# A two-block model on one core: output quarters of the second block's mixers in another order, and how the first expert pieces are released

## The reference, cut to what matters

```
h = h + hybrid_mixer(rms_norm(h, g1), w_in, ..., w_out, lb)     # ends in: concat(r_out, h_out) @ w_out  (1024 x 1024)
h = h + expert_choice_ffn(rms_norm(h, g2), w_router, w_gate, w_up, w_down)

def expert_choice_ffn(xn, w_router, w_gate, w_up, w_down):      # 16 experts, each takes 32 tokens
    affinity = softmax(xn @ w_router)
    gate, idx = top_k(swapaxes(affinity, 1, 2), 32)
    xe = xn[idx]
    ye = (silu(xe @ w_gate) * (xe @ w_up)) @ w_down * gate
    return zeros.at[idx].add(ye)
```

## Time and profile before

| | us |
|---|---|
| median of three runs | 1857.3 (1857.11 to 1859.0) |
| profiled execution, its own time | 1856.24 |
| its span, first to last instruction | 1854.4 |

### The profile page before, as it was taken

How to read it: one execution, slowest core, us unless ns; L and a number is a source line. 1 busy time by engine, 2 the same in 40 slices (tenths; PEclk the granted TensorE clock), 3 DMA queues, 4 the chain that set the end, 5 groups by cost and what they waited for, 6 DMA issues and landing times.

```text
span 1854.4 us, 24842 instructions
## 1 busy us (share of the span) xinstructions
PE 1454.0 (78%) x10541; PEld 1069.3 (58%) x10541; DVE 799.2 (43%) x1246; ACT 571.2 (31%) x898; POOL 62.2 (3%) x56
## 2 busy tenths in 40 slices
PE   8999999999999999985555445579999555555546
PEld 7999999989999898861212112149886121111212
DVE  5767777776777799830101001019973010000101
ACT  4655555465554585321000000028532100000001
POOL 1010000010000000100000000002010000000000
PEclk9999999999999999998777778789999877777868
DMA  9426555534655385799999999997479999999997
GB/s 325 145 70 226 191 174 173 171 104 154 199 182 182 110 271 161 294 372 430 429 430 430 430 429 429 430 394 245 153 293 369 430 429 429 430 430 429 430 429 315
DMA packets 165492, 563.14 MB, mean 304 GB/s; under 512 B 12600, under 2 KB 116534, under 8 KB 137606
## 3 DMA queue, kind: packets, MB, share of 16 engines
q1 hardware_dynamic: 155318, 551.49, 76.2%
q10 hardware_dynamic: 10064, 10.06, 1.8%
HBM read 558.05 MB, written 1.05 MB: 301 GB/s over the span
## 4 chain that ended last, share of the span: by engine, by line
PE 54%; issue 23%; DMA 17%; DVE 3%; ACT 2%; POOL 1%; SPq 0%; POOLq 0%; PEldq 0%; ACTq 0%; DVEq 0%
PE psum L2682 6%; PE psum L2721 5%; PE psum L2976 5%; PE psum L2659 5%; PE psum L2661 5%; PE psum L2660 5%; DMA ring<-in_w_down 5%; DMA ring<-in_w_up 3%; DMA arena<-in_w_gate 3%; PE psum L2711 3%; PE psum L2831 2%; PE psum L2958 2%; PE psum L2576 2%; DMA arena<-in_w_down 2%; DMA arena<-in_w_up 2%
## 5 line engine op out<-in xcount | busy, mean ns | idle before, releaser
L2976 PE MATMUL psum<-ring,arena 128*32 128x512 f32 (+1 forms) x1600 | 280.6, 691 | 198.4 <-DMA ring<-in_w_down 77.8
L2976 PE MATMUL psum<-arena 128*32 128x512 f32 x1024 | 207.6, 702 | 149.5 <-DMA ring<-in_w_up 40.3
L2976 PEld LDWEIGHTS psum<-ring,arena 128*32 128x32 f32 x1600 | 70.7, 128 | 346.0 <-issue 343.4
L907 DVE TENSOR_TENSOR W<-ring,W 128x2048 fp32r<-128x2048 f32 (+1 forms) x92 | 206.3, 2243 | 85.1 <-ACT W L888 84.5
L2274 DVE TENSOR_TENSOR arena<-arena,psum 128x512 f32<-128x512 f32 x16 | 11.0, 690 | 452.7 <-PE psum L2976 452.7
L2659 PE MATMUL psum<-XT,W 128*128 128x256 f32 x704 | 199.4, 283 | 0.0
L2661 PE MATMUL psum<-XT,W 128*128 128x256 f32 x704 | 199.1, 283 | 0.0
L2660 PE MATMUL psum<-XT,W 128*128 128x256 f32 x704 | 199.0, 283 | 0.0
L888 ACT ACTIVATE W<-ring 128x2048 fp32r<-128x2048 f32 (+1 forms) x92 | 172.3, 1872 | 78.7 <-PE psum L2661 42.5
L2976 PEld LDWEIGHTS psum<-arena 128*32 128x32 f32 x1024 | 50.5, 127 | 251.4 <-issue 251.4
L2660 PEld LDWEIGHTS psum<-XT,W 128*128 128x128 f32 x704 | 134.9, 192 | 0.9
(11 more groups left out here) (341 smaller groups left out, 2619.0 us busy)
## 6 DMA issues: line engine op xcount, KB each, us to landing
ring<-in_w_down SPq DMA_DIRECT2D x36, 2048.0 KB, 30.0
ring<-in_w_up SPq DMA_DIRECT2D x32, 2048.0 KB, 31.2
ring<-in_w_up SPq DMA_DIRECT2D x58, 1024.0 KB, 5.1
ring<-in_w_gate SPq DMA_DIRECT2D x28, 2048.0 KB, 33.5
ring<-in_w_in SPq DMA_DIRECT2D x54, 1024.0 KB, 7.6
arena<-in_w_up SPq DMA_DIRECT2D x24, 2048.0 KB, 32.9
arena<-in_w_down SPq DMA_DIRECT2D x20, 2048.0 KB, 29.9
arena<-in_w_gate SPq DMA_DIRECT2D x20, 2048.0 KB, 29.8
```

The costliest lines, as they stand in the source:

```text
L907: nc.vector.tensor_tensor(W2[split_pair(v)][:, c], slot(v % SLOTS_1)[:, c], W1[split_pair(v)][:, c].bitcast(F32), ALU.subtract).then_inc(r ...
L2976: last = nc.tensor.matmul(psum[CAP * e:CAP * (e + 1), b, 0:cols.stop - cols.start], src[:, 4 * half + k, CAP * e:CAP * (e + 1)], tiles[e][ ...
```

## The change

Six edits in the second model's layers, none in what is computed but the sign in the third.

- Order of the output products: 0, 1, 2, 4, 5, 6, 3, 7, with `out_w1` buffers 0, 1, 2, 3, 0, 1, 2, 0. ACT and DVE still prepare 0 to 7 with 3 moved behind 6 on DVE. Product 7 is cut by tokens: its first 128 tokens go to bank 7, its last 128 to bank 5 (product 3 likewise), with adding, turning and logits of the last quarter by token halves, and the logits of quarters 1 and 2 moved ahead of product 7 and between its halves.
- A quarter's slot is released by the last matmul that reads it, not by `release`. Home 6 waits for product 3; homes 5 and 7 and n = 20 for the end of product 7. SP's order becomes 17, 18, 19, 14, 13, 15, 20, 21, 7.
- The router's weights are no longer negated on POOL; the maximum is taken and negated in one DVE instruction, and the exponentials use the positive scale. One DVE instruction (L2225) is gone.
- n = 22 and 23 are loaded as two halves each (one of the two rows that a partition holds, 512 KB). The first quad frees the first row of slots 0 and 1 after its first round over k, the second row at its end. SP issues the first halves of both, then the second halves.
- The last of four one-hot instructions (tokens 128 to 255, 12 experts) moves behind the first two scalings; PE waits for it ahead of the second gather.
- The products' matmul order is first x first, first x rest, rest x first.

```
-OUT_HOMES = {5: (18, 2), 6: (19, 4), 7: (19, 4)}
+OUT_HOMES = {6: (19, None), 5: (19, 5), 7: (19, 5)}
+OUT_BUFFER = [0, 1, 2, 3, 0, 1, 2, 0]
+OUT_ORDER = [0, 1, 2, 4, 5, 6, 3, 7]
+OUT_BANK = [(4, 4), (5, 5), (6, 6), (7, 5)]
+RAW_BANK = [(0, 0), (1, 1), (2, 2), (3, 6)]
+BY_HALF_SLOTS = (22, 23)
...
-            return out_w1[:, SLOT_W // 2 * (n % 4):SLOT_W // 2 * (n % 4 + 1)]
+            return out_w1[:, SLOT_W // 2 * OUT_BUFFER[n]:SLOT_W // 2 * (OUT_BUFFER[n] + 1)]
...
+                def half_slot(s, src, j):
+
+                    sp.wait_ge(slot_free[s], j + 1)
+                    if j == 1:
+                        sp.sem_clear(slot_free[s])
+                    sp.dma_start(slot(s)[:, j * D:(j + 1) * D], src[:, j, :]).then_inc(slot_loaded[s], 16)
...
-                        sp.wait_ge(logits, past(logits) + 1)
+                        sp.wait_ge(wo_mm, past(wo_mm) + 5)
...
-                                if n != ISSUED_LAST:
+                                if n in BY_HALF_SLOTS:
+                                    if n == BY_HALF_SLOTS[0]:
+                                        for other in (e, e + 1):
+                                            half_slot(single_home(lay, g, mat, pair, other)[0], src[other], 0)
+                                    half_slot(s, src[e], 1)
+                                elif n != ISSUED_LAST:
                                     first_group_piece(s, i, src[e])
                                 for home in [h for h in OUT_HOMES if OUT_HOMES[h][0] == n]:
-                                    sp.wait_ge(wo_mm, past(wo_mm) + OUT_HOMES[home][1])
+                                    if OUT_HOMES[home][1]:
+                                        sp.wait_ge(wo_mm, past(wo_mm) + OUT_HOMES[home][1])
+                                    else:
+                                        sp.wait_ge(proj2, past(proj2) + len(ITEMS) + 4)
...
-                pool.tensor_scalar(wr[:, :, :], wr[:, :, :], -1.0, None, ALU.mult).then_inc(gated, 1)
...
+                    elif n == 7:
+                        act.wait_ge(wo_mm, past(wo_mm) + 1)
...
-                squares(act, BY_COLUMNS, lambda i: (x_mid, past(x_mid) + i // TT + 1), sumsq)
-
-                act.wait_ge(scaled, past(scaled) + TT)
+                squares(act, BY_COLUMNS, lambda i: (x_mid, past(x_mid) + (i // TT + 1 if i < 3 * TT else i - TT)), sumsq)
+
+                act.wait_ge(scaled, past(scaled) + 1)
...
+                    last = nc.scalar.activation(elog[:, t], psum[:, 4, t * EXPERTS:(t + 1) * EXPERTS], ACT.Exp, scale=rs[:, t:t + 1],
...
-                rest_of_out(3)
...
-                for n in range(4, 8):
+                for n in OUT_ORDER[3:]:
...
+                def turn_raw_dve(i, t=None):
+
+                    dve.wait_ge(turned, past(turned) + 9 + i + 1 + (t or 0))
                     gain = par2[:, C2_N2 + 2 * i:C2_N2 + 2 * i + 2]
-                    nc.vector.tensor_tensor(raw_turned[:, 2 * i:2 * i + 2, :], psum[:, i, :].rearrange("p (k s) -> p k s", k=2),
-                                            gain.unsqueeze(2).broadcast_to([P, 2, S]), ALU.mult).then_inc(xt_dve, 1)
+                    tokens = slice(0, S) if t is None else slice(t * P, (t + 1) * P)
+                    nc.vector.tensor_tensor(raw_turned[:, 2 * i:2 * i + 2, tokens],
+                                            psum[:, RAW_BANK[i][t or 0], :].rearrange("p (k s) -> p k s", k=2)[:, :, tokens],
+                                            gain.unsqueeze(2).broadcast_to([P, 2, tokens.stop - tokens.start]),
+                                            ALU.mult).then_inc(xt_dve, 1)
...
-                for i in range(4):
+                for i in range(3):
                     dve.wait_ge(wo_mm, past(wo_mm) + i + 1)
                     dst = X[:, :, 256 * i:256 * (i + 1)]
                     nc.vector.tensor_tensor(dst, psum[:, 4 + i, :].rearrange("p (t n) -> p t n", t=TT), dst,
                                             ALU.add).then_inc(x_mid, 1)
                     if i:
                         turn_raw_dve(i - 1)
-                turn_raw_dve(3)
+                turn_raw_dve(2)
+
+                def add_last(t):
+
+                    dve.wait_ge(wo_mm, past(wo_mm) + 3 + t + 1)
+                    dst = X[:, t, 768:1024]
+                    nc.vector.tensor_tensor(dst, psum[:, OUT_BANK[3][t], t * S:(t + 1) * S], dst, ALU.add).then_inc(x_mid, 1)
+
+                add_last(0)
+                turn_raw_dve(3, 0)
+                add_last(1)
+                turn_raw_dve(3, 1)
...
-                dve.wait_ge(rms, past(rms) + 2)
-                nc.vector.tensor_scalar(linv, rs, -1.0, None, ALU.mult).then_inc(scaled, 1)
                 dve.wait_ge(logits, past(logits) + 1)
                 lg = psum[:, 4, 0:TT * EXPERTS].rearrange("p (t e) -> p t e", t=TT)
-                nc.vector.tensor_reduce(lmax, lg, AX.X, ALU.min).then_inc(soft, 1)
+                nc.vector.tensor_reduce(lmax, lg, AX.X, ALU.max).then_inc(soft, 1)
+                dve.wait_ge(rms, past(rms) + 2)
                 dve.wait_ge(soft, past(soft) + 1)
-                nc.vector.tensor_tensor(lmax, lmax, rs, ALU.mult).then_inc(scaled, 1)
+                nc.vector.scalar_tensor_tensor(out=lmax, in0=lmax, scalar=-1.0, in1=rs, op0=ALU.mult, op1=ALU.mult).then_inc(scaled, 1)
...
+                for t in range(TT):
+                    one_hot_rows(0, GROUP, t)
+                one_hot_rows(GROUP, EXPERTS, 0)
...
+                    if g == 0:
+                        one_hot_rows(GROUP, EXPERTS, 1)
...
-                def project_half(n):
+                def project_half(n, t):
                     i, ks = n % 4, range(4, 8) if n < 4 else range(4)
-                    pe.wait_ge(rest, past(rest) + N_IN2 - SPLIT_FROM + n + 1)
+                    if t == 0:
+                        pe.wait_ge(rest, past(rest) + N_IN2 - SPLIT_FROM + OUT_ORDER.index(n) + 1)
                     w1 = out_first(n).rearrange("p (k n) -> p k n", k=4)
                     w2 = rounded_slot[mixer_slot(lay, N_IN2 + i)][:, out_half(n)].rearrange("p (k n) -> p k n", k=4)
+                    for k in ks:
+                        if i == t == 0 and k % 2 == 0:
+                            pe.wait_ge(xt_rest, past(xt_rest) + 1 + {4: 1, 6: 2, 0: 3, 2: 4}[k])
+                        if n == 7 and t == 1 and k == 2:
+                            turn_raw(3, 0)
+                        for m, (x, wt) in enumerate(((mixed_first, w1), (mixed_first, w2), (mixed_rest, w1))):
+                            last = nc.tensor.matmul(psum[:, OUT_BANK[i][t], t * S:(t + 1) * S], x[:, k, t * P:(t + 1) * P], wt[:, k % 4, :],
+                                                    start=((t == 0 or i == 3) and k == 4 and m == 0), stop=(k == 3 and m == 2),
+                                                    skip_group_check=True)
+                            if (t, k, m) == (TT - 1, 3, 1):
+                                last.then_inc(slot_free[mixer_slot(lay, N_IN2 + i)], 1)
+                    return last
+
...
-                for i in range(4):
-                    project_half(i).then_inc(proj2, 1)
-                    if i == 1:
-                        pe.wait_ge(mix_done, past(mix_done) + 2 * TT)
-                        for nth, b in ((2, 0), (3, 1)):
-                            turn_half(nth, b)
-                for i in range(4):
-                    project_half(4 + i).then_inc(wo_mm, 1)
-                    release(wo_mm, past(wo_mm) + i + 1, [mixer_slot(lay, N_IN2 + i)])
+                for n in range(2):
+                    both_tokens(n).then_inc(proj2, 1)
+                pe.wait_ge(mix_done, past(mix_done) + 2 * TT)
+                for nth, b in ((2, 0), (3, 1)):
+                    turn_half(nth, b)
+                both_tokens(2).then_inc(proj2, 1)
+                for i in range(3):
+                    both_tokens(4 + i).then_inc(wo_mm, 1)
                     if i:
                         turn_raw(i - 1)
-                    if i >= 2:
-                        raw_logits(i - 2)
-                release(None, 0, [])
-                turn_raw(3)
+                raw_logits(0)
+                both_tokens(3).then_inc(proj2, 1)
+                turn_raw(2)
+                raw_logits(1)
+                project_half(7, 0).then_inc(wo_mm, 1)
                 raw_logits(2)
-                raw_logits(3).then_inc(logits, 1)
+                project_half(7, 1).then_inc(wo_mm, 1)
+                raw_logits(3, 0)
+                turn_raw(3, 1)
+                raw_logits(3, 1).then_inc(logits, 1)
...
-                            pe.wait_ge(slot_loaded[s], 16)
+                            pe.wait_ge(slot_loaded[s], 16 * pieces)
...
-                                if k == 1 and cols.stop == D and homes[e][1] is None:
+                                if cols.stop == D and homes[e][1] is None and (k == 1 or (g, mat, pair) == (0, 0, 0) and e < 2):
...
```

(55 more changed lines are left out.)

20 lines of the change are left out of this document (5 added, 15 removed).

## The result

| | before | after |
|---|---|---|
| median of 20 runs each, us | 1857.04 (1854.74 to 1859.24) | 1861.14 (1858.16 to 1863.47) |
| profiled execution, its own time | 1856.24 | 1862.39 |
| its span | 1854.4 | 1860.6 |

The ratio is 1.0021 [1.0014, 1.0027]: the change makes the kernel 4.1 us slower (2.6 to 5.0), where 0.4 us faster was forecast.

A forecast was written before the change was run, and what follows sets the result against it. The expert stage was taken as bound by DMA bytes at 430 GB/s, with PE following. Per layer 1.64 - 0.13 - 1.71 = -0.2 us, twice -0.4 us, gave 1856.9 us; 8-in-10 range 1853.0 to 1859.8.

The forecast's parts named there:

- fixed bytes: Ahead of the first expert quad: bytes sendable are fixed, so filling the first two holes widens the third; value nothing.
- holes worth their size: Rival: stream holes between 790 and 820 us count fully, 5.4 us a layer, 1846.5 us; chance 0.06.
- Router's delay: Tail behind product 7: the softmax's bias comes at 806.18 instead of 804.54, 1.64 us later a layer.
- moved one-hot instruction: Ahead of the first quad: scaling starts sooner without the last one-hot row, 0.13 us earlier, bounds 0 and 0.46.
- two stalls: PE waits on DVE for weights 4 (0.29 us) and for the first addition behind weights 7 (0.55): 0.84 us.
- no new stalls: Rival: DVE fits the first addition in and product 4 is not held; 0.80 instead of 1.64, 1855.2 us; chance 0.18.
- a router in time: Rival: the router is not later at all; 1.84 us gained a layer, 1853.6 us; chance 0.12.
- Halves: First quad, n = 22 and 23: first halves issued four rounds sooner, 1.71 us gained a layer, or nothing.
- the restart's price: Stream behind the first quad: starting from empty costs 1.7 us, paid once, the same before and after.
- slower rival: SP's list, 817 to 821: halves give nothing, router's delay shows, +1.5 us a layer, 1860.3 us; chance 0.16.
- doubles of 829.20: Next double loads, issued 1.5 us later: arrival at 832.4 stays hidden by queued pieces, 1.1 us to spare.
- fixed cost for each transfer: Two extra DMAs a layer at about 2.0 us fixed each, if paid in the open: 4 us a layer slower.

The follow-up runs named there:

- whole pieces: Changed kernel with n = 22 and 23 loaded whole behind the first quad's end and six more idle PE products a layer: 1859.51 us, 1.0012.
- late halves: Kernel before with n = 22 and 23 as four 512 KB transfers, none issued ahead of the first quad's end: 1859.44 us, 1.0016.
- after with six idle products: Changed kernel with six more unread PE products a layer in the waits for the choice of tokens: 1860.00 us, 1.0020.
- quarters: Kernel before with n = 22 and 23 as four 256 KB transfers each, behind the first quad's end, and six more idle products: 1860.54 us, 1.0019.
- doubles by rows: Kernel before, second group's first gate quad's four doubles each as four 4 KB-row transfers in a full queue, six more idle products: 1858.40 us, 1.0006.
- early halves alone: Kernel before with only the early-issued halves of n = 22 and 23: 1859.00 us, 1.0014; with six more idle products 1858.33 us, 1.0006.
- kernel before with six idle products: Kernel before with six more unread PE products a layer in the waits for the choice of tokens: 1856.77 us, 1.0000.

## Why the prediction was wrong

- **What bounds it, fixed bytes: right.** The stage runs at 430 GB/s before and after, the hole near 790 went to 804 and beyond, and the release alone is worth nothing (1.0001). The rival of holes worth their size is out.
- **Router's delay: right.** 1.67 us at the first quad against 1.51 forecast, with each landmark within 0.2 us. Most of the difference is the moved one-hot instruction: the softmax's bias is 1.67 us late as well, so it brought nothing where 0.13 was taken. The two stalls are worth 0.6 (0.84 forecast). The rivals of no new stalls and of a router in time are out. With whole pieces the stream loses 1.8 us a layer.
- **Halves: the step that failed.** I took the issue's 1.71 us as the stream's gain, with the restart's price "before and after alike". The issue did come as forecast. But behind a restart the stream did not run at 430 GB/s on transfers of 512 KB: 1.0 us is lost (1.6 with 256 KB), so that 0.8 us a layer is gained in the 53 us where 1.71 was taken, and 0.2 to 0.3 by the end of the expert stage. The sum of -0.2 a layer becomes +1.0 in the 53 us and, from first output product to first output product and from there to the end of the span, +1.4 and +2.0, all in the execution without a fall. I had named "nothing, if the small start runs dry" as the bound; in the 53 us the halves came half way to it, over the layer nearly all the way. The slower rival, with the halves giving nothing (1860.3), was the nearest, though not by its mechanism: the shares of 0.94 to 0.98 with late halves show a slow stream, not one that stops.
- **The doubles of 829.20: right.** They left 1.67 us later and the stream did not notice.
- **A fixed cost for each transfer: not seen.** Two more transfers cost 1.0 us a layer behind the restart, twelve more 0.4 to 0.5 us where the queue is full, so there is no one price for a transfer. The Trainium skill ("DMA: Bandwidth & Descriptors", section "Anatomy of one DMA") gives about 2.0 us fixed for each DMA, on the path where GpSimd issues it. By an estimate from that figure two more would cost 4 us a layer in the open; these are issued by SyncE, and the runs do not agree.
- **Not in the sum at all: the end of a layer.** The last store takes 0.6 us more, by the number of transfers; and in the layers of after with six idle products the last expert product ends 0.6 and 0.4 us later than the loss says. Kernels with halves in the second layer have its last weight bytes 0 to 1.8 us later than the loss says, those with whole pieces or quarters 0.2 at most. Why is open.

Together 2 x 1.0 in the 53 us of the two layers, 1.0 behind them and 0.6 for the store make 3.6 us, against 3.4 measured in that execution and 2.6 to 5.0 in the ratio. The rest to 4.1 us is not settled. Falls of the clock are one candidate (they also came in kernels with nothing changed ahead of the quad: it was 1.2 us late in a layer of the doubles by rows, and the profiled execution of after has one). The loss behind the 53 us is largest for early halves alone (1.0014 and 1.0006): in the first layer of that kernel with six idle products, without a fall, the stream is 0.5 us ahead, but the next layer's first product comes 604.83 us behind this one's, 1.0 us more than before.

## What to carry to other kernels

When a refill is cut to start it sooner, count the stream's rate behind the start as well as the start: here a cut that led an empty queue lost half of its gain while only small transfers were in it, and most of the rest by the end of the layer. Compare whole layers, not only the stretch that was changed. Where the bytes ahead of a dependent step are fixed, holes in front of it are worth nothing and only the step's own time counts. If a transfer must be cut, try shorter rows before fewer partitions: here 1.0 us a layer against about 5.

## What the runs showed of the hardware

- Where the queue is full a packet of 4 KB takes 159 ns (doubles by rows) and behind the restart one of 8 KB 309 ns (kernel before with six idle products), medians, nearly the same rate. In the 4 us behind the restart with late halves the 4 KB packets took 180 to 187 ns on average at shares of 0.94 to 0.98, so most of that loss is in slower packets; with quarters it is in gaps as well (share 0.73).
- Two transfers of 64 partitions instead of one of 128, two pieces a layer: about 5 us a layer, and packets of 8 KB that take 632 ns.
- The last store of 512 KB takes 3.5 or 4.1 us by how many transfers the program held before it (four more than the kernel before, or 0, 2, 6, 12, 24). What in that number matters is open.
- The granted clock fell to 0.50 for 3.4 us between the logits and the end of the first quad in 17 of 40 profiled layers, at different places in one kernel's two layers, and made the first quad 0.2 to 1.4 us late; six products more in the waits did not stop it.
